# Layer 1 of a two-layer hybrid encoder: the prompt halves of the first u block are issued between the last groups of the indexer's dots

## The chip, the cores and the metric

The kernel runs on one core of a Trainium2 chip. The metric is the device time of one execution in microseconds, the median of several runs. Before the change three runs gave 1494.12 us (1491.05 to 1496.53).

## The reference, cut to what matters

Two layers are run over 512 prompt tokens and 64 sample tokens (the sample has 512 cached keys). Everything is float32. In each layer one input projection gives the queries, keys and values of a sparse attention, the queries and keys of an indexer, and `u`, which feeds a convolution module:

```python
proj = h @ w_in
q, k, v, iq, ik, iw, u = jnp.split(proj, SPLIT_POINTS, axis=-1)
a, b = jnp.split(u, 2, axis=-1)
g = a * jax.nn.sigmoid(b)                       # GLU
dots  = jnp.einsum('bqhd,bsd->bqhs', qi, ik_all)     # 8 indexer heads
score = jnp.einsum('bqhs,bqh->bqs', jax.nn.relu(dots), wi)
top_val, top_idx = lax.top_k(score, k_top)      # attention runs over these keys alone
y = conv(padded g, conv_w)                      # causal, depthwise, width 31
x = x + gate * (concat(attention, swish(layer_norm(y))) @ w_out)
```

After the mixer comes a mixture of 16 experts (1024 to 256 to 1024), which the change doesn't touch. The outputs are y and the new keys, values, indexer keys and convolution states.

## The kernel before, in words

The program is written by hand, engine by engine: each engine has its own list of instructions, carried out in the order written, and semaphores join the lists. There is no planner. Where an instruction of one engine waits, all that is written behind it on that engine waits too.

The five token tiles are four of 128 prompt tokens (t = 0 to 3) and one of 64 sample tokens (t = 4). `hT` holds the normed input, transposed; `W` is a ring of six slots of 1 MB for weights, filled by SyncE (SP, `load`) as TensorE (PE) gives slots back (`used` marks a slot, and the next matmul that has no semaphore of its own to raise carries the release). PSUM has eight banks, `ps[0]` to `ps[7]`.

The stage around the change, in layer 1 (l = 1):

1. **Dots (L572 to L591 on PE).** 32 steps n = 0 to 31, eight heads for each of the tiles 4, 3, 2, 1. Step n writes one of the banks 5, 6, 7 (and, for tile 4, n < 8, the new keys' part into bank 3 or 4), for which `pe.wait_ge(L["rel"], n - 2)` must have passed. ScalarE (ACT) takes each with a Relu (L1029) once the score of step n - 3 is in, and VectorE (DVE) adds it into the scores (L1406 for a tile's first head, L1409 for the rest). Steps come in groups of four, g = n // 4. After the last step of the groups 1 to 5 PE issues `project_q`, one token tile of the query projection (8 matmuls of 512 columns), into the banks 0 to 2. In the same places ACT squares the query rows and takes roots, and DVE sums them, inverts, and does `select(3)`, three rounds of the search for the 8 largest scores (MAX8 L1369, MATCH_REPLACE8 L1370). 66 rounds are due in all (18, 16, 16 and 16 for the tiles 4, 3, 2, 1), 21 of them inside this stage.
2. **u blocks (`u_block`, L598).** The 1024 columns of u make four blocks i of 128 channels of a and b. A block has four products of 8 matmuls each: the prompt tokens' a and b (512 columns; banks 3 and 4 for an even i, 5 and 6 for an odd one), then the sample tokens' a and b (64 columns, bank 7). Blocks 0 and 1 begin when all 32 Relus are done (`pe.wait_ge(L["rel"], 32)`). The sample products of block i >= 1 wait until the GLU of block i - 1 is done (`s_glu`, L609). Each product raises `uproj` when it ends.
3. **GLU.** ACT's `gates(i)` takes the sigmoid of b (L1058 for the prompt, L1061 for the sample). DVE's loop `for i, rounds in enumerate((10, 12, 18, 100))` first does that many rounds of selection and then multiplies (L1437, L1438), which raises `s_glu`.
4. **Shifted copies.** SP's `shifted(i)` waits for `s_glu` and issues 16 DMAs (L395) that lay block i out for the convolution in `G4[i % 2]`.
5. **Convolution (`conv`, L615, matmuls L623).** `conv(i)` waits for these 16 DMAs (L617), for the tap matrices that GpSimd built, and for ACT's copy of conv(i - 1) (L1067).

PE's order is: dots, u 0, u 1, conv 0, u 2, conv 1, u 3, conv 2, some transposes, conv 3, then the turned queries, the layer norm's sums and the attention.

SP's order is: the loads of w_in, the two loads of w_out's first half, `shifted(0)` to `shifted(3)`, the two loads of w_out's second half, and then the experts' weights.

Of the kernel before, what the change touches and what calls it, by code (L numbers as in the profile page):

```python
# [24 lines left out]
P = 128  # L25
DEPTH = 2
D = 1024
KC = D // P
SEQ, DEC, PAST = 512, 64, 512
# [45 lines left out]
def rows_of(t):  # L75
    return P if t < 4 else DEC
# [22 lines left out]
def program(nc, A, O):  # L99
    ctx = ExitStack()  # L100
    with ctx:
        def sb(name, shape, dt=F32):
            return ctx.enter_context(nc.sbuf_tensor(name, shape, dt))

        def sem(name):
            return ctx.enter_context(nc.semaphore(name))
# [5 lines left out]
        W = sb("W", [P, 6, 2048])  # L112
        C = sb("C", [P, NCONST])
        X = sb("X", [P, NT, D])
        hT = sb("hT", [P, KC, TOK])
# [72 lines left out]
        ps = [ctx.enter_context(nc.psum_tensor(f"ps{i}", [P, 512], F32)) for i in range(8)]  # L188
# [39 lines left out]
        L = {n: sem("l_" + n) for n in names}  # L228
# [31 lines left out]
        def mixer_use(l, c, hf):  # L260

            if l == 1:
                return MIX1 + 2 * c + hf
            return (MIX0 + 2 * c, MIX0 + 2 + 2 * (c - 1), MIX0 + 4, U_Q, U_U0, U_U1, U_OUT0, U_OUT0 + 2)[c] + hf
# [16 lines left out]
        def keys_of(t):  # L281

            return (0, NKEYS[t]) if t < 4 else (512, 1024)
# [176 lines left out]
        def _(pe):  # L460
# [4 lines left out]
            def count(ins, done):  # L465

                if done is not None:
                    ins.then_inc(done, 1)
                elif done_units:
                    ins.then_inc(w_free[done_units.pop(0)], 1)  # L470

            def products(out, pairs, done=None, before=None, halfway=None):
                for n, (l, r) in enumerate(pairs):
                    if before is not None and n == len(pairs) // 2:
                        before()
                    ins = T.matmul(out, l, r, start=n == 0, stop=n == len(pairs) - 1, skip_group_check=True)  # L476
                    if halfway is not None and n == len(pairs) // 2:
                        assert not done_units
                        done_units.append(halfway)
                    count(ins, done if n == len(pairs) - 1 else None)  # L480
# [8 lines left out]
            def came(use):  # L489
                pe.wait_ge(w_ld[use % 6], (use // 6 + 1) * 16)  # L490

            def used(use):
                done_units.append(use % 6)
# [6 lines left out]
            def ada(out, first_use, steps, third):  # L500

                for k in steps:
                    use = first_use(k) if third == 2 else first_use + k
                    came(use)
                    for j in range(4):
                        ins = T.matmul(out[32 * j:32 * j + 32, :], scT[:, k, :], W[:, use % 6, 512 * j:512 * j + 512],  # L506
                                       start=k == 0, stop=k == KC - 1, skip_group_check=True)
                        count(ins, s_ada if k == KC - 1 and j == 3 else None)
                    used(use)
# [5 lines left out]
            for l in range(DEPTH):  # L515
# [18 lines left out]
                def tokens(t):  # L534
                    return slice(t * P, t * P + rows_of(t))

                def project(c, n, job, t, first, last):

                    us = [mixer_use(l, c, q) for q in range(2)]
                    wv = [W[:, us[q] % 6, 0:4 * n].rearrange("p (k c) -> p k c", c=n) for q in range(2)]  # L540
                    if job >= 3:
                        pe.wait_ge(L["proja"], job - 2)
                    if first:
                        came(us[0])
                    products(ps[job % 3][0:rows_of(t), 0:n], [(hT[:, k, tokens(t)], wv[k // 4][:, k % 4, :]) for k in range(KC)], L["proj"],
                             before=(lambda: came(us[1])) if first else None, halfway=us[0] % 6 if last else None)
                    if last:
                        used(us[1])
# [22 lines left out]
                def project_q(n):  # L571
                    project(3, 512, 15 + n, ATTN[n], n == 0, n == NT - 1)  # L572

                for n, (t, h) in enumerate((t, h) for t in SCORED for h in range(8)):
                    if n >= 3:
                        pe.wait_ge(L["rel"], n - 2)
                    hp = slice(64 * (h % 2), 64 * (h % 2) + 64)
                    a, b = keys_of(t)
                    q = qT[hp, h // 2, tokens(t)]
                    if t == 4:  # L580
                        if n >= 2:
                            pe.wait_ge(L["rel"], n - 1)
                        count(T.matmul(ps[3 + n % 2][0:DEC, 0:DEC], q, kT[0][hp, 1024:1088], start=True, stop=True), None)
                    count(T.matmul(ps[5 + n % 3][0:rows_of(t), 0:b - a], q, kT[0][hp, a:b], start=True, stop=True), L["dots"])  # L584
                    if l == 0 and n % 2 == 1:
                        third, k = divmod(n // 2, KC)
                        if k == 0:
                            pe.wait_ge(L["proja"], 15)
                        ada(ps[1 - third], (U_ADA1, U_ADA2)[third], [k], third)
                    if l == 1 and n % 4 == 3 and 1 <= n // 4 <= 5:  # L590
                        project_q(n // 4 - 1)  # L591
                if l == 0:
                    pe.wait_ge(s_adae, 3)
                    for n in range(NT):
                        project_q(n)

                def u_block(i):  # L598

                    c = 4 + i // 2  # L600
                    pe.wait_ge(*((s_glu, 4 * l + i - 1) if i >= 2 else (L["rel"], 32)))
                    for ab, smp in ((0, 0), (1, 0), (0, 1), (1, 1)):
                        at = P * (i % 2) + ab * DEC
                        out = ps[7][:, at:at + DEC] if smp else ps[3 + 2 * (i % 2) + ab][:, 0:SEQ]
                        tk = slice(SEQ, TOK) if smp else slice(0, SEQ)
                        if i % 2 == 0 and not smp:
                            came(mixer_use(l, c, ab))
                        if i >= 1 and smp and ab == 0:
                            pe.wait_ge(s_glu, 4 * l + i)  # L609
                        wv = W[:, mixer_use(l, c, ab) % 6, :].rearrange("p (k c) -> p k c", c=256)  # L610
                        products(out, [(wv[:, k, (i % 2) * P:(i % 2) * P + P], hT[:, k, tk]) for k in range(KC)], L["uproj"])
                        if i % 2 == 1 and smp:
                            used(mixer_use(l, c, ab))
# [21 lines left out]
                def turn_q(n):  # L635
# [5 lines left out]
                    turn([(ps[(5, 6, 3, 4, 7)[n]][:, i * m:(i + 1) * m], qkf[0:m, t, i * P:(i + 1) * P]) for i in range(4)], L["tq"])  # L641

                u_block(0)
                ada3(0)
                u_block(1)
                ada3(1)
                conv(0)
                u_block(2)
                ada3(2, 3)
                conv(1)  # L650
# [215 lines left out]
                with pe.If_ne(further, 0):  # L866
                    pe.wait_ge(L["ya"], NE)
                    pe.wait_ge(L["yd"], NE)
                    with pe.Fori(0, pe.snap(further, min_val=0, max_val=XJ)):
# [5 lines left out]
                        for s in range(2):  # L875
                            wv = JW[s].rearrange("p (k f) -> p k f", f=DE)
# [961 lines left out]
```

## Time and profile before

| what | value |
|---|---|
| runs, median (lowest to highest) | 1494.12 us (1491.05 to 1496.53) |
| the profiled execution's own time | 1492.04 us |
| its span, first to last instruction | 1490.2 us |
| PE busy | 1258.9 us (84%) |
| VectorE busy | 548.7 us (37%) |
| ScalarE busy | 368.6 us (25%) |
| GpSimd busy | 151.9 us (10%) |
| mean granted TensorE clock | 0.904 of full |
| the stage of this change in layer 1 | about 862 us to 1044 us |

### The profile page before, as it was taken

The numbers are of one execution on the slowest core, as the hardware profiler recorded it, in microseconds if no ns is written. First come the engines' busy times: TensorE is split into PE (matmuls) and PEld (weight loads), VectorE is DVE, ScalarE is ACT, GpSimd is POOL, SyncE is SP. The second block draws the span as 40 slices with busy tenths as digits, with TensorE's granted clock in tenths as the row PEclk, the third lists the DMA queues.
The fourth block names the chain that finished last, engine by engine and source line by source line (L and its number), as shares of the span: only waits on it lengthen the run. The fifth ranks groups of instructions, "written<-read, shape, count | busy, mean of one in ns | idle before, by whom it ended". The sixth has DMA issues, their size and how long they took to land.

```text
span 1490.2 us, 16205 instructions
## 1 busy us (share of the span) xinstructions
PE 1258.9 (84%) x6299; PEld 739.5 (50%) x6299; DVE 548.7 (37%) x1394; ACT 368.6 (25%) x838; POOL 151.9 (10%) x218
## 2 busy tenths in 40 slices
PE   4998799987899879999709987998787995999980
PEld 0572244543445467777505733544455454777750
DVE  1106689023345521111151058960423454211114
ACT  2124110035741111111131142001468111111113
POOL 0401050010000160000021014110100011000002
PEclk9998899987999879999958989999858996999995
DMA  9248996261950589999560310224030026799975
GB/s 362 63 146 290 363 332 201 72 228 35 312 184 34 189 289 371 365 362 368 179 230 0 123 59 29 72 66 138 20 76 3 1 97 206 254 363 362 366 248 190
DMA packets 137126, 284.99 MB, mean 191 GB/s; under 512 B 11565, under 2 KB 91861, under 8 KB 130649
## 3 DMA queue, kind: packets, MB, share of 16 engines
q1 hardware_dynamic: 116416, 209.70, 41.9%
q0 software_dynamic: 8352, 42.50, 8.2%
q10 hardware_dynamic: 12281, 31.74, 6.0%
q8 instruction: 50, 0.82, 0.2%
q14 instruction: 27, 0.22, 0.0%
HBM read 237.91 MB, written 52.40 MB: 195 GB/s over the span
## 4 chain that ended last, share of the span: by engine, by line
PE 69%; DVE 11%; DMA 7%; ACT 6%; issue 4%; SPq 1%; ACTq 1%; POOL 0%; DVEq 0%; POOLq 0%
PE ps L476 46%; PE ps L765 9%; PE ps L486 5%; PE ps L623 3%; PE ps L684 3%; DMA W<-in_w_gate 2%; ACT arena L1106 2%; DMA X<-in_x_sample 2%; SPq L395 1%; DVE arena L1409 1%; PE ps L506 1%; DVE arena L1460 1%; PE ps L584 1%; DVE arena L1370 1%; DMA arena<-y_d,sid 1%
## 5 line engine op out<-in xcount | busy, mean ns | idle before, releaser
L476 PE MATMUL ps<-W,arena 128*128 128x256 f32 (+1 forms) x1280 | 345.5, 426 | 8.2 <-ACT arena L1212 2.8
L476 PEld LDWEIGHTS ps<-W,arena 128*128 128x128 f32 x1280 | 240.9, 192 | 82.8 <-issue 53.8
L476 PE MATMUL ps<-W,hT 128*128 128x512 f32 (+5 forms) x640 | 197.2, 468 | 6.3 <-DVE gt L1289 6.3
L486 PE MATMUL ps<-C,arena 128*128 128x128 f32 (+3 forms) x851 | 125.3, 292 | 61.5 <-DMA arena<-x_d 14.4
L476 PEld LDWEIGHTS ps<-W,hT 128*128 128x128 f32 (+1 forms) x640 | 103.4, 183 | 100.2 <-issue 86.4
L486 PEld LDWEIGHTS ps<-C,arena 128*128 128x128 f32 (+3 forms) x851 | 102.7, 155 | 97.8 <-issue 31.6
L765 PE MATMUL ps<-W,hT 128*128 128x512 f32 (+1 forms) x320 | 144.8, 607 | 5.7 <-ACT hT L1163 5.7
L476 PE MATMUL ps<-hT,W 128*128 128x64 f32 (+1 forms) x512 | 142.6, 440 | 7.1 <-ACT arena L1029 7.1
L476 PEld LDWEIGHTS ps<-hT,W 128*128 128x128 f32 x512 | 79.0, 193 | 72.1 <-issue 64.2
L765 PEld LDWEIGHTS ps<-W,hT 128*128 128x128 f32 (+1 forms) x320 | 57.1, 184 | 80.0 <-issue 73.6
L1672 DVE TENSOR_TENSOR arena<-arena,ps 128x256 f32<-128x256 f32 x32 | 13.5, 421 | 213.9 <-ACT arena L1204 213.9
L1369 DVE MAX8 small<-arena 64x8 f32<-64x576 f32 (+3 forms) x132 | 80.5, 610 | 3.7
L1370 DVE MATCH_REPLACE8 arena<-small,arena 64x576 f32<-64x576 f32 (+3 forms) x132 | 78.4, 594 | 0.0
L623 PE MATMUL ps<-arena 128*32 128x64 f32 (+1 forms) x1024 | 66.5, 418 | 5.6 <-DMA arena<-arena 5.6
L506 PE MATMUL ps<-W,scT 128*32 128x512 f32 x384 | 59.9, 723 | 9.8 <-DMA W<-in_w_ada 9.4
L1774 POOL DMA_INDIRECT x_d<-arena,sid x30 | 28.8, 960 | 379.1 <-DVE sid L1582 366.2
L684 PE MATMUL ps<-arena 64*128 64x128 f32 (+4 forms) x160 | 57.0, 631 | 10.9 <-DVE small L1460 10.5
L1802 POOL DMA_INDIRECT arena<-y_d,sid x20 | 19.5, 975 | 399.2 <-DMA y_d<-arena 201.0
L1204 ACT ACTIVATE arena<-ps 128x256 f32<-128x256 f32 x32 | 12.3, 384 | 189.4 <-PE ps L476 189.4
L1106 ACT ACTIVATE arena<-arena,small 128x128 f32<-128x128 f32 (+4 forms) x80 | 47.3, 593 | 45.1 <-DVE small L1472 45.1
L1667 DVE COPY arena<-ps 128x512 f32<-128x512 f32 x32 | 22.1, 691 | 93.1 <-PE ps L476 93.1
L1460 DVE CUSTOM_DVE_ANT_0 arena<-ps,arena 64x512 f32<-64x512 f32 (+3 forms) x64 | 35.9, 587 | 55.4 <-PE ps L684 54.8
(244 smaller groups left out, 1112.1 us busy)
## 6 DMA issues: line engine op xcount, KB each, us to landing
W<-in_w_ada SPq DMA_DIRECT2D x48, 1024.0 KB, 7.0
W<-in_w_gate SPq DMA_DIRECT2D x32, 1024.0 KB, 10.6
W<-in_w_up SPq DMA_DIRECT2D x32, 1024.0 KB, 13.0
W<-in_w_down SPq DMA_DIRECT2D x32, 1024.0 KB, 7.6
arena<-x_d SPq DMA_DIRECT2D x33, 512.0 KB, 11.1
y_d<-arena ACTq DMA_DIRECT2D x33, 512.0 KB, 7.2
W<-in_w_in SPq DMA_DIRECT2D x16, 1024.0 KB, 8.4
arena<-arena SPq DMA_DIRECT2D x128, 79.2 KB, 2.1
```

Source lines behind the costliest of these rows:

```text
L476: ins = T.matmul(out, l, r, start=n == 0, stop=n == len(pairs) - 1, skip_group_check=True)
L486: count(T.transpose(o, i, ident[0:m, 0:m]), done if n == len(outs_ins) - 1 else None)
L506: ins = T.matmul(out[32 * j:32 * j + 32, :], scT[:, k, :], W[:, use % 6, 512 * j:512 * j + 512], start=k == 0, stop=k == KC - 1, skip_grou ...
L623: ins = T.matmul(ps[b][32 * g:32 * g + 32, 0:n], W4[:, i % 2, NQ * g + q, :], G4[i % 2][:, g, s0 + 4 * q:s0 + 4 * q + n], start=q == 0, st ...
L684: T.matmul(ps[logit_bank(job)][0:rows_of(t), 0:b - a], q, kT[1][hp, a:b], start=True, stop=True).then_inc(L["lgt"], 1)
L765: ins = T.matmul(ps[5 + n % 3][0:rows_of(t), :], hT[:, 4 * q + k, tokens(t)], wv[:, k, :], start=q == 0 and k == 0, stop=last, skip_group_ ...
L1106: ins = S.activation(r, r, ACT.Exp, bias=small[0:m, q:q + 1], accum_out=small[0:m, h:h + 1])
L1369: chain(V.max(m8, sc))
L1370: chain(V.match_replace(sc, m8, sc, MARK))
L1460: ins = V.tensor_tensor_reduce(r[:, 0:k], ps[logit_bank(job)][0:m, 0:k], mk[:, 0:k], 0.125, MARK, ALU.add, ALU.max, small[0:m, mx:mx + 1])
L1667: V.tensor_copy(ys[:, u, 512:1024], ps[7][:, :]).then_inc(L["yd"], 1)
L1774: G.indirect_dma_start(out=x_d[:, :], out_offset=bass.IndirectOffsetOnAxis(ap=table[0:m, 5 * k + t:5 * k + t + 1], axis=0), in_=HR[0:m, t, ...
```

## The change

In layer 1 the two prompt products of u block 0 (a into bank 3, b into bank 4) are issued inside the loop over the dots: a after step 23, behind the last `project_q`, and b after step 27. `u_block(0)` then leaves out its prompt products in layer 1 and issues only the sample's. Layer 0 is as before, and so are all the other engines' lists.

```diff
                     if l == 1 and n % 4 == 3 and 1 <= n // 4 <= 5:
                         project_q(n // 4 - 1)
+                    if l == 1 and n in (23, 27):
+                        ab = n // 4 - 5
+                        came(mixer_use(l, 4, ab))
+                        wv = W[:, mixer_use(l, 4, ab) % 6, :].rearrange("p (k c) -> p k c", c=256)
+                        products(ps[3 + ab][:, 0:SEQ], [(wv[:, k, 0:P], hT[:, k, 0:SEQ]) for k in range(KC)], L["uproj"])
...
                         tk = slice(SEQ, TOK) if smp else slice(0, SEQ)
+                        if l == 1 and i == 0 and not smp:
+                            continue
                         if i % 2 == 0 and not smp:
                             came(mixer_use(l, c, ab))
```

## Rows read from the trace of the kernel before

**Rows 1.** The page: the span, the busy times, the chain by engine.
```profile
span 1490.2 us, 16205 instructions
PE 1258.9 (84%) x6299; PEld 739.5 (50%) x6299; DVE 548.7 (37%) x1394; ACT 368.6 (25%) x838; POOL 151.9 (10%) x218
PE 69%; DVE 11%; DMA 7%; ACT 6%; issue 4%; SPq 1%; ACTq 1%; POOL 0%; DVEq 0%; POOLq 0%
```

**Rows 2.** The chain that ended last: start, duration, engine, tile, line.
```profile
930.98 37.61 PE ps L476 x128
968.59 7.90 PE ps L623 x128
976.49 17.45 PE ps L476 x64
993.94 7.90 PE ps L623 x128
1001.84 17.46 PE ps L476 x64
...
1031.21 2.12 DMA arena<-arena
```

**Rows 3.** Timeline of PE at the end of the dots.
```profile
912.80 7.13 PE L476 MATMUL ps<-W,hT 128*128 128x512 f32 x16
919.86 1.13 PE L584 MATMUL ps<-arena 64*128 64x256 f32 x6
921.64 2.22 PE L584 MATMUL ps<-arena 64*128 64x256 f32 x10 [0.65 <-ACT arena L1029]
930.98 37.61 PE L476 MATMUL ps<-hT,W 128*128 128x512 f32 x128 [7.12 <-ACT arena L1029]
```

**Rows 4.** Timeline of DVE: selection, scores and the GLU products.
```profile
919.69 0.73 DVE L1370 MATCH_REPLACE8 arena<-small,arena 64x576 f32<-64x576 f32 x1
921.69 0.35 DVE L1406 TENSOR_SCALAR arena<-arena,iw 128x256 f32<-128x256 f32 x1 [1.27 <-ACT arena L1029]
929.97 2.25 DVE L1409 SCALAR_TENSOR_TENSOR arena<-arena,iw 128x256 f32<-128x256 f32 x4
952.15 0.69 DVE L1437 TENSOR_TENSOR arena<-ps,arena 128x512 f32<-128x512 f32 x1
952.76 0.21 DVE L1438 TENSOR_TENSOR arena<-ps,arena 128x64 f32<-128x64 f32 x1
969.93 0.22 DVE L1438 TENSOR_TENSOR arena<-ps,arena 128x64 f32<-128x64 f32 x1
994.30 0.69 DVE L1437 TENSOR_TENSOR arena<-ps,arena 128x512 f32<-128x512 f32 x1 [4.13 <-ACT arena L1061]
```

**Rows 5.** Timeline of ACT: Relus, then the sigmoids of blocks 0, 1 and 2.
```profile
921.22 0.91 ACT L1029 ACTIVATE arena<-ps 128x256 f32<-128x256 f32 x3
930.55 0.38 ACT L1029 ACTIVATE arena<-ps 128x256 f32<-128x256 f32 x1 [6.26 <-DVE arena L1409]
947.81 0.60 ACT L1058 ACTIVATE arena<-ps 128x512 f32<-128x512 f32 x1 [14.94 <-PE ps L476]
990.46 0.60 ACT L1058 ACTIVATE arena<-ps 128x512 f32<-128x512 f32 x1 [13.01 <-PE ps L476]
```

**Rows 6.** Timeline of SP: loads of w_in, the 16 issues of shifted(0) and of shifted(1).
```profile
826.90 29.25 SPq L373 DMA_DIRECT2D W<-in_w_in  x6
...
953.00 10.04 SPq L395 DMA_DIRECT2D arena<-arena  x16
970.18 11.32 SPq L395 DMA_DIRECT2D arena<-arena  x16
```

**Rows 7.** Timeline of PE: conv 3 of layer 0 and of layer 1.
```profile
308.44 7.97 PE L623 MATMUL ps<-arena 128*32 128x512 f32 x128 [1.42 <-DMA arena<-arena]
1033.38 10.75 PE L623 MATMUL ps<-arena 128*32 128x512 f32 x128 [4.14 <-DMA arena<-arena]
```

**Rows 8.** Windows: length, busy PE, PEld, DVE, ACT, POOL, then PEclk, DMA share, GB/s.
```profile
924.00:926.00 2.00, 0.00 (x0) 0.00 (x0) 1.93 (x6) 0.28 (x1) 1.04 (x1) 1.00 0.00 0
928.00:930.00 2.00, 0.00 (x0) 0.00 (x0) 1.90 (x5) 0.00 (x0) 1.09 (x4) 0.50 0.00 0
934.00:936.00 2.00, 2.00 (x3) 0.72 (x3) 1.93 (x4) 0.00 (x0) 1.92 (x5) 0.50 0.80 223
...
1029.00:1031.00 2.00, 0.24 (x2) 0.10 (x1) 0.00 (x0) 0.95 (x3) 0.00 (x0) 1.00 0.45 119
```

## The prediction, made before the run

> **What bounds the kernel now.** I read the page first: over a span of 1490.2 us PE is busy 84% and the chain that ended last lies on PE for 69% [rows 1]. Then I followed that chain through layer 1's dots, u blocks and convolutions. From 930.98 to 1019.3 us it is PE without a break: blocks 0 and 1 together 37.61 us, conv 0 7.90, block 2 17.45, conv 1 7.90, block 3 17.46 [rows 2]. So in this stretch PE's own work sets the end, and whatever starts it later moves the end.
>
> Two losses stand just ahead of it. PE is idle 7.12 us between its last dots (921.64 + 2.22 = 923.9) and block 0 [rows 3], and it wakes at half clock: the granted clock is 1.00 at 924 to 926, 0.50 at 928 to 930, still 0.50 at 934 to 936 while PE is fully busy [rows 8]. The prompt products of block 0 took 947.75 - 930.98 = 16.8 us (ACT's first sigmoid begins at 947.81, some 0.06 after their end), those of block 2 at full clock 990.40 - 976.49 = 13.9 us [rows 2, 5]. So the cold start costs 2.9 us, and one product of 8 matmuls costs 6.95 us warm.
>
> Who makes PE idle there? Not PE's own queue but VectorE: the last Relu (930.55) had waited 6.26 us for a score [rows 5], and DVE does three rounds of selection before it reaches the scores of the last group at 929.97 [rows 4]. DVE goes on without a pause from 921.69 to the end of the GLU product of block 0 at 952.97 [rows 4]. The second line to watch therefore is DVE, then SP, then conv 0: SP starts the 16 issues of shifted(0) at 953.00 and needs 10.04 us [rows 6], the last transfer of such a set takes 2.12 us more [rows 2], so conv 0's data is there at 965.2 us, and conv 0 begins at 968.59 [rows 2]. This line has only 3.4 us to spare.
>
> **The change part by part.**
>
> *What moves.* 16 matmuls (32 records) of 512 columns, no DMA and no work of another engine. Removed from block 0: 16.8 us on PE. Added after step 23 and after step 27: 6.95 us each. Their weights are in: SP issued the last six loads of w_in between 826.90 and 856.2 [rows 6]. The banks 3 and 4 were last used in the steps of tile 4, n < 8. A side effect is that the release of the last query weights' slot, which before had to wait for block 0's first matmul, is now carried at 920 us, so one 1 MB load of w_out starts some 11 us earlier, at a time when SP has nothing else to do. I cost it at nothing: its data is used after the attention.
>
> *The first product against the dots of group 6.* PE ends the last project_q at 912.80 + 7.13 = 919.9 [rows 3]. The three dots that follow take 1.13 us, 0.38 each [rows 3]. With the product ahead of them the first ends at 919.93 + 6.95 + 0.38 = 927.3. Its Relu began at 921.22 before (ACT was busy with the squares until then) [rows 5] and now begins at 927.3: +6.1. DVE has finished its selection at 920.4 (919.69 + 0.73) and had the first score of the group at 921.69 [rows 4]; now it gets it at 927.8. DVE had no other work there, so it stands idle about 7 us instead of 1.27, and since it runs without a pause from 921.69 to 952.97, all that follows on it is 6.1 us late. This is the point of the whole change: the moved matmuls fill PE's gap of 7.12 us only after having cut the supply of the engine that made the gap.
>
> *The second product against group 7.* The dots of group 6 are out at 928.4, the product ends at 935.35, the next dots at 935.7, their Relu at 936.2. DVE reaches that score at 929.97 + 6.1 = 936.1 on its own. So it is at most 0.2 us more, and DVE's delay is 6.3 us. This product is hidden; but only because the first already delayed DVE.
>
> *PE after the dots.* The last Relu ends 6.3 us later, at 937.2. Then PE has block 0's sample products, 3.5 us (993.94 - 990.40 [rows 2, 5]), to 940.7, and block 1's prompt products, 13.9 us, to 954.6. For PE alone that is some 10 us ahead of before (968.59 - 3.5 = 965.1). But block 1's sample products wait for the GLU of block 0, which now ends at 952.97 + 6.3 = 959.3. PE idles 4.7 us there, does them (3.5 us, or up to 7 cold), and at 963 to 966 waits again, for conv 0's data: 959.3 + 10.07 + 2.12 = 971.5 us. Nothing can go round this, since SP issues behind `s_glu` and PE takes conv 0 ahead of block 2. Conv 0 begins 971.5 - 968.59 = 2.9 us later than before.
>
> *Its clock.* This idle time is 5.5 us or more, after another of 4.7. Layer 1's conv 3 came after 4.14 us of idle and took 10.75 us; layer 0's came after 1.42 us and took 7.97 [rows 7]. The idle time of conv 0 is longer than the first, so I take the full 2.8 us (bounds 0 and 2.9, the latter from block 0's own cold start, which the change saves, a saving that stands already in the 6.95 us a product).
>
> The Trainium skill ("TensorE: Matmul & The Clock Gate", Part 1) says that the throttled clock is the default and that activity releases it. Read for the gap at 924 alone this rule speaks for the change: work in the gap keeps the clock up. The rows agree (0.50 after the gap), but the rule applies as well to the two gaps which the change opens further on; by the first alone the sum would be 2.8 us less.
>
> *After conv 0.* Block 2 needs the GLU of block 0, there long before. Conv 1's data: the second GLU ends at 970.15 + 6.3 = 976.5 [rows 4], plus 11.32 + 2.12 [rows 2, 6] = 989.9, conv 1 begins near 999.6. DVE's selection for block 2 ended 4.13 us before its sigmoid came [rows 4]; it comes 5.7 later and DVE is 6.3 later, so the margin is still 3.5 us. From here to the end all that is left is PE's chain, shifted as it stands; the experts' loads start from slots that PE frees and move with it.
>
> *The sum.* +2.9 (data of conv 0) + 2.8 (its cold clock) = +5.7 us. The profiled execution took 1492.04 us (span 1490.2); it would take 1497.7. It lies 2.1 us under the median of the runs, 1494.12. I give the forecast against the median: 1494.1 + 5.7 = 1499.8 us.
>
> **The rivals.**
>
> *A. Faster: PE fills its gap.* PE's own account says 10 us less before conv 0. Even if DVE weren't late at all, conv 0's data would be there no sooner than 965.2, so the most is 3.4 us faster, and with a cold conv 0 (PE would then have waited from about 956.5, 3.5 us after the GLU of block 0 at 952.97) 0.6. For it: PE's gap of 7.12 us is real. Against it: Relus, scores and dots are in strict order and DVE's reserve at 920.4 is 1.27 us. Break-even is at a DVE delay of 3.4 us warm, 0.6 cold, where I find 6.3. Time 1490.7 to 1493.5.
>
> *B. The clock stays up at conv 0.* If the sample products between the two gaps keep it, conv 0 takes 7.9: +2.9, 1497.0.
>
> *C. More than 7.5 us slower.* Mechanism: SP's 16 issues. Those of shifted(1) took 11.32 us against 10.04 [rows 6]; if one of the slow kind falls into shifted(0) it adds 1.3 (+7.0), and a half-clocked start of block 2 after a cold conv 0 would add up to 1 more: 1501 to 1502.5.
>
> *D. Nothing.* If PE's dots were ready anyway while the products run, nothing would move at DVE; then A's figure holds.
>
> **How the numbers follow.** Forecast (+5.7, with small parts either way, 1498 to 1501.5) 0.6; B 0.15; C 0.2; A with D 0.05. What a measurement of this kernel can tell from no change is about 0.5%, 7.5 us. The forecast (0.38%) lies inside it, B too; from C nearly all, and of the forecast a few in a hundred through the scatter of medians (the three runs spread over 5.5 us), come out above. So faster 0.03, within 0.75, slower 0.22. The range is 1495.5 to 1504.5: it takes in B and C and the scatter, and leaves out A.
>
> **What would show it.** In the trace after: PE without its 7 us gap at 924 but the product at about 920 to 927; the first score of group 6 at 927.8 and DVE idle about 7 us before it; the GLU product of block 0 ending at 959.3, SP's issues behind it; PE idle 4 to 5 us inside block 1 and 5 us or more before conv 0; conv 0 at 971.5, 10.7 us long with a granted clock of 0.50. It is wrong if the first Relu of group 6 still begins near 921, if the GLU of block 0 ends before 956, or if conv 0 starts before 968.6.

## The result, and the profile after

16 runs each: 1500.14 us (1496.22 to 1504.48) with the change, 1494.24 us (1490.67 to 1496.61) before. The ratio is 1.0041, 95% interval 1.003 to 1.0053: slower by 6.1 us (4.5 to 7.9). That is clear of the scatter, but its middle lies under the 0.5% that was taken as the bound of no change. The forecast was 1499.8 us, +5.7.

The profiled execution of the changed kernel has a span of 1501.2 us, 11.0 more. Not all of that is the change: the last `project_q`, up to which both kernels do the same, starts at 912.80 before [rows 3] and at 917.48 after. This start is scatter: in the twelve traces of this document it lies between 912.80 and 918.64. So times below are counted from the start of that record, T = 912.80 before and T = 917.48 after.

Timeline of PE after the change (start, duration, line, operation, idle time before it); it answers to [rows 3]:

```profile
917.48 7.13 PE L476 MATMUL ps<-W,hT 128*128 128x512 f32 x16
924.45 7.03 PE L476 MATMUL ps<-hT,W 128*128 128x512 f32 x16
931.41 1.87 PE L584 MATMUL ps<-arena 64*128 64x256 f32 x8
933.20 7.13 PE L476 MATMUL ps<-hT,W 128*128 128x512 f32 x16
940.27 1.87 PE L584 MATMUL ps<-arena 64*128 64x256 f32 x8
942.61 20.89 PE L476 MATMUL ps<-hT,W 128*128 128x64 f32 x64 [0.47 <-ACT arena L1036]
964.53 3.79 PE L476 MATMUL ps<-hT,W 128*128 128x64 f32 x32 [1.03 <-DVE arena L1445]
977.11 10.30 PE L630 MATMUL ps<-arena 128*32 128x512 f32 x128 [8.80 <-DMA arena<-arena]
987.34 17.52 PE L476 MATMUL ps<-hT,W 128*128 128x512 f32 x64
...
1030.14 7.97 PE L630 MATMUL ps<-arena 128*32 128x512 f32 x128
```

PE's gap of 7.12 us is gone, and the two products stand among the dots. Instead PE waits 8.80 us for conv 0's data (line numbers behind the edit are 7 higher, so L630 is the convolution, L623 before). DVE and SP, against [rows 4, 6]:

```profile
932.63 0.35 DVE L1413 TENSOR_SCALAR arena<-arena,iw 128x256 f32<-128x256 f32 x1 [7.53 <-ACT arena L1036]
...
941.48 2.25 DVE L1416 SCALAR_TENSOR_TENSOR arena<-arena,iw 128x256 f32<-128x256 f32 x4 [0.60 <-ACT arena L1036]
...
963.65 0.69 DVE L1444 TENSOR_TENSOR arena<-ps,arena 128x512 f32<-128x512 f32 x1
964.26 0.21 DVE L1445 TENSOR_TENSOR arena<-ps,arena 128x64 f32<-128x64 f32 x1
```
```profile
964.50 11.09 SPq L395 DMA_DIRECT2D arena<-arena  x16
```

DVE waits 7.53 us for the first score of group 6 (1.27 before [rows 4]) and 0.60 for that of group 7 (none before). Its GLU product ends at T + 47.0 instead of T + 40.2, SP's issues follow at once (964.50), and conv 0 starts at T + 59.6 instead of T + 55.7. The chain of waits now runs that way too: DVE from 941.48 to 964.50, SP to 975.0, where it starts the last issue, 2.07 us from there to the landing, then PE.

| from T, in us | before | after | difference |
|---|---|---|---|
| GLU of block 0 ends | 40.2 | 47.0 | +6.8 |
| conv 0 starts | 55.7 | 59.6 | +3.9 |
| block 2 starts | 63.6 | 69.9 | +6.2 |
| conv 2 starts | 106.4 | 112.7 | +6.2 |

### The profile page after: what moved, and what is told of

Same layout as the page of the kernel before. It is cut to its first block, busy times and chain, and to the rows that moved or that the text cites. A ratio compares the mean times of both kernels' runs of the same rounds, so it can differ in the third digit from the quotient of the medians.

```text
span 1501.2 us, 16204 instructions
## 1 busy us (share of the span) xinstructions
PE 1261.6 (84%) x6299; PEld 738.8 (49%) x6299; DVE 549.4 (37%) x1394; ACT 368.9 (25%) x838; POOL 152.1 (10%) x218
## 4 chain that ended last, share of the span: by engine, by line
PE 68%; DVE 12%; DMA 7%; ACT 5%; issue 4%; SPq 2%; ACTq 1%; POOL 0%; DVEq 0%; POOLq 0%
PE ps L476 44%; PE ps L772 9%; PE ps L486 5%; PE ps L630 3%; PE ps L691 3%; DMA W<-in_w_gate 2%; ACT arena L1113 2%; SPq L395 2%; DMA X<-in_x_sample 2%; DVE arena L1377 1%; DVE small L1376 1%; PE ps L584 1%; DVE arena L1416 1%; PE ps L506 1%; DVE arena L1467 1%
## 5 line engine op out<-in xcount | busy, mean ns | idle before, releaser
L1679 DVE TENSOR_TENSOR arena<-arena,ps 128x256 f32<-128x256 f32 x32 | 13.5, 421 | 215.8 <-ACT arena L1211 215.8
L630 PE MATMUL ps<-arena 128*32 128x64 f32 (+1 forms) x1024 | 67.5, 422 | 13.7 <-DMA arena<-arena 13.7
```

What stands on the lines that cost most here:

```text
L630: ins = T.matmul(ps[b][32 * g:32 * g + 32, 0:n], W4[:, i % 2, NQ * g + q, :], G4[i % 2][:, g, s0 + 4 * q:s0 + 4 * q + n], start=q == 0, st ...
```

## The experiments

Each was timed in five rounds beside the kernel before; its times are compared with the runs of before taken with it. "Conv 2 starts" is counted from T in its own trace and is 106.4 us in the kernel before; the column behind it is the difference from these 106.4 us.

| kernel | conv 0 starts | conv 2 starts | conv 2, against before | timed ratio (95%) |
|---|---|---|---|---|
| the change | 59.6 | 112.7 | +6.2 us | 1.0041 (1.003 to 1.0053) |
| late | 52.7 | 105.9 | -0.5 | 0.9996 (0.9982 to 1.0011) |
| double | 66.5 | 119.5 | +13.1 | 1.0098 (1.0073 to 1.0122) |
| third | 53.6 | 106.4 | 0.0 | 0.9982 (0.9965 to 0.9999) |
| after_rounds | 53.7 | 106.3 | -0.1 | 0.9997 (0.9982 to 1.0012) |
| warm | 59.6 | 110.3 | +3.8 | 1.003 (1.0015 to 1.0045) |
| after_u2 | 64.6 | 102.2 | -4.2 | 0.9964 (0.9948 to 0.998) |
| before_u2 | 69.5 | 106.5 | +0.1 | 0.9997 (0.9977 to 1.0016) |
| late_u2 | 59.5 | 96.5 | -9.9 | 0.9925 (0.9902 to 0.9948) |
| late_u2b, the same kernel again | 59.5 | 96.5 | -9.9 | 0.9941 (0.9921 to 0.9961) |
| late_u2_tq | 59.5 | 96.5 | -9.9 | 0.9909 (0.9886 to 0.9932) |

### Where the products stand: late, double, third

late:

```diff
-                    if l == 1 and n in (23, 27):
-                        ab = n // 4 - 5
+                    if l == 1 and n == 31:
+                      for ab in range(2):
```

> The two prompt products of block 0 stand behind step 31 of the dots, without the wait for the last Relu, instead of behind steps 23 and 27. Theory (the first product starves VectorE because the dots are issued in order behind it; VectorE, then SyncE's 16 issues, set the start of conv 0): no dots stand behind the products, so VectorE is as in the kernel before, the GLU product of block 0 ends 40.2 us after the start of the last project_q (before 40.2, changed kernel 47.0); conv 0 starts where its data is there, 52.5 to 53.5 us after that point (before 55.7, changed 59.6), with a cold clock (10.2 to 10.7 us long). Sum against the kernel before: -2.8 + 2.4 = about -0.4 us, that is 5.5 to 6.5 us faster than the changed kernel. Rival 1 (PE's own account counts): some 10 us faster than before. Rival 2 (moving the products costs by itself, by clock or weight loads, wherever they stand): as slow as the changed kernel, +6 us.

Measured 1493.46 us beside 1493.07, DVE's GLU product 40.2 us after T as in the kernel before. PE goes from the dots (926.38 + 2.22) straight into the products, all dots being out already:

```profile
917.54 7.13 PE L476 MATMUL ps<-W,hT 128*128 128x512 f32 x16
924.61 1.13 PE L584 MATMUL ps<-arena 64*128 64x256 f32 x6
926.38 2.22 PE L584 MATMUL ps<-arena 64*128 64x256 f32 x10 [0.65 <-ACT arena L1036]
928.53 34.83 PE L476 MATMUL ps<-hT,W 128*128 128x512 f32 x128
970.21 10.48 PE L630 MATMUL ps<-arena 128*32 128x512 f32 x128 [6.85 <-DMA arena<-arena]
```

The theory holds and both rivals fall. The same work in the same gap costs nothing once no dots stand behind it. It brings next to nothing either: conv 0 starts 3.0 us sooner than in the kernel before, as soon as its data is there, but runs cold (10.48 us), which takes back 2.5.

double (the same edit with `n == 23`):

> Both prompt products stand behind step 23, none behind step 27: the same work in the same stage, but twice as long ahead of the dots of group 6. Theory: VectorE's delay doubles, from 6.8 to 13.0 to 13.8 us, the GLU product of block 0 ends 53 to 54 us after the start of the last project_q, conv 0 starts 10 to 11 us later than in the kernel before, cold: +12 to +13.5 us against the kernel before. Rival (the time is lost by the clock or by the number of interruptions, not by VectorE's starvation): one interruption less, so no slower than the changed kernel, +6 us or less.

Measured 1507.68 us beside 1493.07 (+14.6, by the ratio). DVE waits 14.40 us, and its GLU product ends 53.3 us after T:

```profile
920.16 13.90 PE L476 MATMUL ps<-hT,W 128*128 128x512 f32 x32
933.99 3.39 PE L584 MATMUL ps<-arena 64*128 64x256 f32 x16
944.51 25.82 PE L476 MATMUL ps<-hT,W 128*128 128x64 f32 x96 [7.12 <-ACT arena L1036]
979.68 10.30 PE L630 MATMUL ps<-arena 128*32 128x512 f32 x128 [9.35 <-DMA arena<-arena]
```
```profile
935.21 0.35 DVE L1413 TENSOR_SCALAR arena<-arena,iw 128x256 f32<-128x256 f32 x1 [14.40 <-ACT arena L1036]
```

Two products ahead of group 6 cost DVE 13.1 us, one costs 6.3 (6.8 with the one behind step 27), and conv 2 starts 13.1 and 6.2 us later. The timed loss of 14.6 us (10.9 to 18.2, six runs) is more than the 12 to 13.5 that were expected; its interval takes them in. PE's own gap of 7.12 us is back as well, since PE waits there for DVE, which does its selection first; PE has work enough behind it.

third:

```diff
-                    if l == 1 and n in (23, 27):
-                        ab = n // 4 - 5
+                    if l == 1 and n == 27:
+                        ab = 0
...
-                        if l == 1 and i == 0 and not smp:
+                        if l == 1 and i == 0 and not smp and ab == 0:
```

> Only the product behind step 27 is moved (it computes the a half; the b half is issued in block 0 as before), nothing behind step 23. Theory: the dots of group 6 are not held up, those of group 7 only by what the product lasts beyond VectorE's selection: VectorE is 0.5 to 1.5 us late instead of 6.8, the GLU product of block 0 ends 40.7 to 41.7 us after the start of the last project_q, conv 0 starts at 53 to 54.5, cold: -1 to +1 us against the kernel before. Rival (each product put among the dots costs the same): half of the changed kernel's loss, +3 us.

Measured 1493.51 us beside 1494.93; GLU product at T + 40.7, conv 0 at T + 53.6 and 10.1 us long. DVE's waits for the first scores of groups 6 and 7:

```profile
923.32 0.35 DVE L1413 TENSOR_SCALAR arena<-arena,iw 128x256 f32<-128x256 f32 x1 [1.28 <-ACT arena L1036]
...
932.16 2.25 DVE L1416 SCALAR_TENSOR_TENSOR arena<-arena,iw 128x256 f32<-128x256 f32 x4 [0.60 <-ACT arena L1036]
```

Only 0.6 us of DVE's time goes. So the two places are not alike: 6.3 of the 6.8 us that VectorE lost belong to the product behind step 23. The timed difference, -2.7 us by the ratio (-5.2 to -0.1), is more than the -1 to +1 that was expected; the trace shows no gain at conv 2. Conv 3 ends 2.1 us sooner than in the trace of before, counted from T, but it does so in before_u2 as well (2.0), whose timing shows no gain (0.9997). What the timed gain is, if it is one, stays open.

### The way from VectorE to conv 0: after_rounds

```diff
-                for i, rounds in enumerate((10, 12, 18, 100)):
+                for i, rounds in enumerate((10, 12, 18, 100) if l == 0 else (6, 16, 18, 100)):
```

> The changed kernel, but in layer 1 VectorE does 6 rounds of selection ahead of the GLU product of block 0 and 16 ahead of that of block 1, instead of 10 and 12 (the sum is the same). Four rounds of 1.52 us are 6.1 us. Theory: the GLU product of block 0 ends 40.9 us after the start of the last project_q instead of 47.0, conv 0 starts at about 53.5 instead of 59.6, after 3 to 4 us of idle PE, so partly cold: 6 to 8.5 us faster than the changed kernel, between -2.4 and 0 us against the kernel before. Rival (the loss lies on PE itself and VectorE is beside the path): no gain, +6 us.

Measured 1492.29 us beside 1493.07. Putting off four rounds, which touches nothing on PE, takes back all that the change had cost. The GLU product ends at T + 40.9, and conv 0 starts at T + 53.7:

```profile
967.90 9.96 PE L630 MATMUL ps<-arena 128*32 128x512 f32 x128 [4.11 <-DMA arena<-arena]
```

This shows the path DVE, SP, conv 0 from its other end. (The kernel before with the same rounds put off was not run; there PE was busy until conv 0 [rows 2].)

### The cold conv 0: warm

```diff
+                if l == 1:
+                    pe.wait_ge(L["proja"], 20)
+                    for _ in range(9):
+                        T.matmul(ps[2][:, 0:SEQ], ident, hT[:, 0, 0:SEQ], start=True, stop=True, skip_group_check=True)
                 conv(0)
```

> The changed kernel with nine matmuls of 512 columns (18 records, about 7.8 us) whose result nobody reads, issued into bank 2 ahead of conv 0 in layer 1, where PE idles 8.8 us. Theory: conv 0 starts at the same time as in the changed kernel (59.6 us after the start of the last project_q), but at full clock, 7.9 us long instead of 10.2: 2.3 us faster than the changed kernel, +3.6 us against the kernel before. Rival (conv 0 is slow for another reason, such as its data or the transfers beside it): no gain, conv 0 stays at 10.2 us.

Measured 1497.65 us beside 1493.07:

```profile
965.62 7.94 PE L657 MATMUL ps<-hT,C 128*128 128x512 f32 x18
974.50 7.97 PE L630 MATMUL ps<-arena 128*32 128x512 f32 x128 [0.94 <-DMA arena<-arena]
```

Conv 0 starts as late as in the changed kernel but takes 7.97 us instead of 10.30. Two windows inside conv 0 (their third value from the end is PEclk), the first of the changed kernel, the second of warm:

```profile
978.00:980.00 2.00, 2.00 (x16) 0.56 (x12) 1.90 (x5) 0.00 (x0) 0.00 (x0) 0.50 0.00 0
...
976.00:978.00 2.00, 2.00 (x24) 0.56 (x20) 1.90 (x6) 0.00 (x0) 0.00 (x0) 1.00 0.00 0
```

So the 6.2 us are 3.9 of late data and 2.3 of clock. This rests on the traces: the timed ratios of the two kernels, 1.003 and 1.0041, have intervals that overlap.

### Where PE's gain went: before_u2, after_u2, late_u2

All three issue block 2's prompt products ahead of conv 0 in layer 1 (`u_block` takes a list of halves); they differ in where block 0's stand.

```diff
+                if l == 1:
+                    u_block(2, (0,))
                 conv(0)
-                u_block(2)
+                u_block(2, (0, 1) if l == 0 else (1,))
```

> A control: the kernel before with block 2's prompt products ahead of conv 0 in layer 1. Theory: PE has no wait between block 0 and conv 2 there, so the order of its work is all that changes: within 1 us of the kernel before. Rival (the other order is itself worth something, by the clock or by the transfers): a gain of 3 us or more, which would then be part of the other two.

> The changed kernel (products behind steps 23 and 27) with block 2's prompt products ahead of conv 0 in layer 1. Theory: the wait of 8.8 us ahead of conv 0 is filled, conv 0 starts at about 64.6 us after the start of the last project_q at full clock, conv 1 at 78 (its data is there at 77.6): the block of convolutions ends some 9 to 10 us sooner than in the changed kernel, that is 3 to 4.5 us faster than the kernel before. Rival (VectorE's delay of 6.8 us stays on the path whatever PE does meanwhile): as slow as the changed kernel, +6 us, or half of it.

> Block 0's prompt products behind step 31 as in the first experiment, and in layer 1 block 2's two prompt products issued ahead of conv 0, in the time in which PE waited 6.85 us for its data. Theory (PE's gain of the early products is real but was lost in that wait): PE goes on without a gap from step 31 to conv 2, conv 0 starts 59.8 us after the start of the last project_q at full clock, conv 1 near 71 instead of 81, conv 3's data some 10 us sooner than before: 8.5 to 10.5 us faster than the kernel before (about 1484). Rival (VectorE's or SyncE's later turns, the second and third GLU or the shifted copies, take over as the bound): conv 1 waits for its data until 75 or more, gain under 5 us.

Measured: before_u2 1493.93 us beside 1494.93, no difference; after_u2 1489.70, -5.4 by the ratio (-7.8 to -3.0); late_u2 1483.57, -11.2 by the ratio (-14.7 to -7.8), and -8.8 when it was run again. PE in late_u2 has no wait from the dots to conv 2:

```profile
925.50 48.61 PE L476 MATMUL ps<-hT,W 128*128 128x512 f32 x160
974.04 7.97 PE L633 MATMUL ps<-arena 128*32 128x512 f32 x128
981.94 3.79 PE L476 MATMUL ps<-hT,W 128*128 128x64 f32 x32
985.65 7.97 PE L633 MATMUL ps<-arena 128*32 128x512 f32 x128
993.55 17.52 PE L476 MATMUL ps<-hT,W 128*128 128x512 f32 x64
1011.00 7.97 PE L633 MATMUL ps<-arena 128*32 128x512 f32 x128
...
1024.77 10.69 PE L633 MATMUL ps<-arena 128*32 128x512 f32 x128 [3.75 <-DMA arena<-arena]
```

The order alone is worth nothing. The early products are worth some 10 us, but only with work in the wait for conv 0's data and with no dots behind them; with dots behind them (after_u2) 4.2 us are left. The 9.9 us are the gap of 7.12 us that PE no longer has and the 2.8 us of its cold start: block 0 to block 2's prompt products took 51.39 us in before_u2 and 48.61 here.

### One step further: late_u2_tq

The four sets of query transposes (`turn_q(0)` to `turn_q(3)`) stand ahead of conv 3 in layer 1, and late_u2 was run again beside it.

> The fastest so far (block 0's prompt products behind step 31, block 2's ahead of conv 0) with the four sets of query transposes (2.07 us on PE) ahead of conv 3 instead of behind it in layer 1, where PE idles 3.75 us and conv 3 then runs cold, 10.69 us long. Theory (a short enough idle time leaves the clock up): two short waits instead of one long one, conv 3 takes 7.9 us, PE's 2.07 us of transposes are hidden: 2.8 to 4.8 us faster than the version without it, 12 to 16 us faster than the kernel before. Rival (the lower clock comes from light work as well as from idle time, and transposes are light work; or the layer norm now waits for ScalarE's copies): 0 to 2 us faster.

> The fastest so far once more, unchanged, as the comparison for the run beside it: 8.5 to 11.5 us faster than the kernel before.

Measured 1481.05 us and 1484.37, beside 1493.30. The layer norm's sums start 121.4 us after T instead of 123.0, so 1.6 us of the hoped-for 2.8 to 4.8. The timed difference is 3.3 us between medians, inside what the theory gave, but from six and eight runs, with ratios whose intervals overlap, so it does not decide between the two. In the trace both causes that the rival named for a smaller gain can be seen, a clock that is low at the start of conv 3 and a wait for ScalarE:

```profile
1021.67 1.85 PE L486 MATMUL ps<-C,arena 128*128 128x128 f32 x13
1024.89 1.94 PE L486 MATMUL ps<-C,arena 128*128 128x128 f32 x8 [1.36 <-ACT arena L1101]
1026.76 8.71 PE L633 MATMUL ps<-arena 128*32 128x512 f32 x128
1037.33 4.51 PE L476 MATMUL ps<-arena,C 128*128 128x512 f32 x16 [1.86 <-ACT arena L1108]
```

Conv 3 takes 8.71 us, not 7.9 (nor 10.65 as in late_u2b), and behind it PE waits 1.86 us for ACT. Still, this version beats both kernels: 0.9909 (0.9886 to 0.9932).

## Why the prediction was right, step by step

- **The first product starves VectorE.** Forecast: first score at T + 15.0, DVE +6.1. Measured: T + 15.15 and a wait of 7.53 instead of 1.27, +6.3. Right, and shown by double (twice) and third (none).
- **The second product adds at most 0.2.** It was 0.6: DVE waited 0.60 us. The product ended at T + 22.9 (933.20 + 7.13) where I had 22.6, and from its end through dots and Relu to the score (941.48) it took 1.15 us where I had 0.9. Small, but the sum's first miss (0.4 us).
- **The GLU at +6.3.** +6.8, by the two above: 0.5 more than forecast.
- **SP's 16 issues and the last transfer.** Two errors here, of opposite sign. The issues were taken at 10.04 us; they took 11.09, since one of them was a long one (1.61 us; most took 0.59), as in `shifted(1)`. The prediction had this as part of rival C, so the first half of C's mechanism came about. And it put the last transfer's 2.12 us behind the end of the last issue, but the trace counts them from its start. This can be seen in the kernel before, where [rows 2] has `1031.21 2.12 DMA` and SP's issues end at 1020.50 + 11.30 = 1031.80:

```profile
1020.50 11.30 SPq L395 DMA_DIRECT2D arena<-arena  x16
```

- **Conv 0 at +2.9.** In that way 0.6 us were counted twice, and the reserve of this line was 4.0 us and not 3.4. From the GLU to conv 0 it took 12.6 us where I had 12.2. With DVE's 0.5 us this makes it +3.9.
- **The cold conv 0.** Taken at 2.8; 2.3 measured (10.23 against 7.90 up to the next start), and warm takes it away. Rival B, the clock staying up, didn't come about.
- **That the total came so close is partly luck.** The mechanism is as forecast, but 0.5 us too little at DVE and 1.0 too little for SP's long issue stand against 0.6 counted twice and 0.5 too much for the clock: +6.2 by conv 2 where +5.7 was forecast.
- **PE between the dots and conv 0.** This was wrong, though it cost nothing. I had 17.4 us warm for the sample products of block 0 and block 1's prompt products and then 4.7 us of idle time. It took 20.9 us and then 1.03: the clock was low there (below). The missing 3.5 us lay in time in which PE would have waited for DVE anyway.
- **After conv 0 everything shifts.** Block 2 to conv 2: right, 42.8 us in both. DVE's margin for block 2 was 3.56 us where I had 3.5. Conv 3 came out 1.3 us shorter than before, and waited 0.7 less, in this one execution (9.48 us after 3.45 of idle time against 10.75 after 4.14 [rows 7]); the rest of the span adds 2.0 again. Conv 3 took 9.30 to 9.53 us in six of the traces and 10.63 to 10.93 in five; the kernel before (10.75) and before_u2 (9.33), which time alike, stand on different sides, so this part looks like scatter. The timed difference of 6.1 fits the 6.2 at conv 2; whether any of the later parts is of the change was not tried.
- **Rival A**, that filling the gap makes it faster, fell as it was put, since DVE was late. Without a delay at DVE (late) it gives -0.5, near the 0.6 that I gave for it with a cold conv 0; with other work for the wait before conv 0 as well (late_u2) it gives -9.9. Rival D, that the dots are ready anyway, fell by DVE's wait of 7.53 us.

## What to carry to other kernels

An idle engine isn't a free place: ask what makes it idle, and what stands behind the new work in its own queue. Here PE idled because VectorE was the slower, and 7 us of matmuls put ahead of the four dots that fed VectorE next cost VectorE 6.3 us; the same matmuls behind the last dots cost nothing. And time gained before a wait is only moved into that wait, where it may cost the clock as well, until there is other work to put there.

## What the hardware showed that was not expected

The granted clock fell while PE was busy. Windows of the changed kernel (length, busy time of PE, PEld, DVE, ACT, POOL, then PEclk, DMA share, GB/s):

```profile
941.00:943.00 2.00, 1.48 (x8) 0.69 (x6) 1.32 (x3) 1.42 (x5) 0.00 (x0) 1.00 0.00 0
943.00:945.00 2.00, 2.00 (x18) 2.00 (x17) 1.83 (x7) 1.82 (x2) 0.99 (x1) 0.83 0.48 148
945.00:947.00 2.00, 2.00 (x11) 2.00 (x10) 1.90 (x5) 0.06 (x1) 1.84 (x4) 0.50 0.00 0
947.00:949.00 2.00, 2.00 (x8) 1.48 (x8) 1.93 (x4) 0.22 (x1) 1.23 (x5) 0.50 0.00 0
949.00:951.00 2.00, 2.00 (x4) 0.94 (x3) 1.90 (x6) 0.00 (x0) 0.00 (x0) 0.50 0.00 0
951.00:953.00 2.00, 2.00 (x5) 0.76 (x4) 1.93 (x4) 0.00 (x0) 0.00 (x0) 0.97 0.00 0
```

PE's longest idle time there was 0.47 us. Ahead of the fall it did dots of 64 x 256 for 1.87 us and then the sample products, 64 columns each, whose weight loads alone fill the time; from about 944 to 951 it ran at 1.2 GHz instead of 2.4. The same stretch took 20.89 to 20.91 us in the three traces with this order of work (the changed kernel, after_u2, warm) and 24.41 in after_rounds with 3.5 us more work in it, so it is no chance of one execution. Block 0's sample products in the kernel before, with products of 512 columns right ahead of them, ran at full clock:

```profile
949.00:951.00 2.00, 2.00 (x20) 2.00 (x20) 1.90 (x5) 0.00 (x0) 0.00 (x0) 1.00 0.00 0
```

In late_u2_tq the transposes of 128 columns, with 1.36 us of idle time among them, ended at 0.50:

```profile
1023.00:1025.00 2.00, 0.64 (x7) 0.47 (x6) 0.00 (x0) 1.19 (x3) 0.00 (x0) 0.97 0.73 177
1025.00:1027.00 2.00, 2.00 (x12) 1.63 (x16) 0.00 (x0) 0.00 (x0) 0.00 (x0) 0.50 0.58 110
```

The Trainium skill ("TensorE: Matmul & The Clock Gate", Part 1) says that the gate is set by how busy TensorE has lately been. By the time that records cover, this trace doesn't bear it out: 2.00 of 2.00 us were covered at 943 to 945, where the clock fell, and at 945 to 947, where it stood at 0.50. Why it fell there, no run here shows.
